# Delta path: keys before queries in the projection, and the scan's first steps of two tiles moved into it

## What is computed

```python
qkv = silu(short_conv(concat([dq, dk, dv]), conv_w))      # 5 taps along the tokens
qd  = l2_norm(heads(cq)) * DN_DK ** -0.5
kd  = l2_norm(heads(ck));  vd = heads(cv)
g    = -exp(a_log) * softplus(da + dt_bias);  beta = sigmoid(db)
# per chunk, for each head and direction
g = cumsum(g);  decay = exp(where(tril, g_i - g_j, -inf))
L = tril(einsum(k_beta, k) * decay, -1)
T = inverse(eye + L)                                      # unit lower triangular
a_intra = einsum(q, k) * decay
v_new = T @ v_beta - (T @ (k_beta * exp(g))) @ state
o     = (q * exp(g)) @ state + a_intra @ v_new
state = state * exp(g_last) + (k * exp(g_last - g)).T @ v_new
```

## Time and profile before

| what | us |
|---|---|
| median of 3 runs (3514.41 to 3517.09) | 3516.15 |
| the profiled execution, its own time | 3511.73 |
| span of that execution | 3509.9 |
| projection, group 0 (2111.8 to 2315.5) | 203.7 |
| scan, group 0, up to the recurrence of tile 0 (2315.6 to 2364.9) | 49.4 |
| one later step of the scan | 26.2 |
| projection, group 1 (2556.5 to 2754.1) | 197.6 |
| scan, group 1, up to the recurrence of tile 0 (2754.2 to 2803.7) | 49.5 |
| busy share of the span: PE, DVE, ACT, POOL | 87%, 59%, 39%, 32% |

### The profile page before, as it was taken

The page is one execution under the profiler, slowest core; times in us unless marked ns, Lnnn a source line. Parts: engine busy times, 40 slices in busy tenths (PEclk is TensorE's granted clock), DMA queues, the critical chain, the costliest instruction groups (busy, mean ns, idle before and its releaser), DMA issues. The chain is left out here.

```text
span 3509.9 us, 44499 instructions
## 1 busy us (share of the span) xinstructions
PE 3069.2 (87%) x16273; PEld 2501.5 (71%) x16273; DVE 2077.2 (59%) x3903; ACT 1377.7 (39%) x2733; POOL 1140.6 (32%) x1254
## 2 busy tenths in 40 slices
PE   5899988878998878899999999868878688899988
PEld 3578756756786657677887887758867588688777
DVE  6699775566997757766761015558755587101333
ACT  1366466124763651336652213434323443221222
POOL 2236321231562224421004332234423344424330
PEclk9999999999998999899999999989989799899999
DMA  6423332621233234310003123022231322512421
GB/s 213 123 79 94 94 96 76 205 104 45 79 97 129 85 113 152 116 37 1 1 10 102 48 83 102 26 76 76 55 109 30 76 80 52 162 48 97 142 96 43
DMA packets 227148, 303.15 MB, mean 86 GB/s; under 512 B 40912, under 2 KB 142032, under 8 KB 224754
## 3 DMA queue, kind: packets, MB, share of 16 engines
q1 hardware_dynamic: 215410, 279.33, 26.1%
q10 hardware_dynamic: 11520, 20.98, 1.6%
HBM read 241.91 MB, written 58.33 MB: 86 GB/s over the span
## 5 line engine op out<-in xcount | busy, mean ns | idle before, releaser
L816 PE MATMUL psum<-qs,hT 128*128 128x512 f32 x1344 | 308.3, 391 | 6.7 <-POOL qs L903 6.6
L816 PEld LDWEIGHTS psum<-qs,hT 128*128 128x128 f32 x1344 | 252.7, 189 | 62.2 <-issue 5.3
L2354 PE MATMUL psum<-bhsn,bringn 128*128 128x512 f32 x1152 | 264.8, 392 | 14.0 <-POOL bringn L2410 13.1
L2667 PE MATMUL psum<-hTs,cws 128*128 128x512 f32 x1056 | 261.0, 409 | 16.5 <-POOL hTs L2922 14.6
L2354 PEld LDWEIGHTS psum<-bhsn,bringn 128*128 128x128 f32 x1152 | 217.8, 189 | 61.0 <-issue 13.5
L2667 PEld LDWEIGHTS psum<-hTs,cws 128*128 128x128 f32 x1056 | 207.5, 198 | 61.4 <-POOL hTs L2922 15.0
L2354 PE MATMUL psum<-bhsa,bringa 128*128 128x512 f32 x1056 | 240.1, 389 | 2.8 <-POOL bringa L2410 2.8
L2354 PEld LDWEIGHTS psum<-bhsa,bringa 128*128 128x128 f32 x1056 | 198.2, 188 | 44.2 <-issue 3.2
L1583 PE MATMUL psum<-w_out,oys 128*128 128x512 f32 x768 | 180.8, 397 | 32.0 <-DVE w_out L1666 29.3
L1583 PEld LDWEIGHTS psum<-w_out,oys 128*128 128x128 f32 x768 | 146.4, 192 | 66.4 <-DVE w_out L1666 30.3
L983 DVE TENSOR_SCALAR_CACHE_REDUCE junk<-score,cand 128x384 uint8<-128x384 f32 x248 | 186.8, 810 | 2.2
(11 more groups left out here) (514 smaller groups left out, 7039.2 us busy)
## 6 DMA issues: line engine op xcount, KB each, us to landing
stg<-in_w_in SPq DMA_DIRECT2D x96, 256.0 KB, 2.7
score<-in_w_ada SPq DMA_DIRECT2D x32, 512.0 KB, 3.8
pj<-ptmp ACTq DMA_DIRECT2D x64, 256.0 KB, 2.1
dlb<-blocks SPq DMA_DIRECT2D x32, 512.0 KB
dlb<-in_w_in SPq DMA_DIRECT2D x22, 512.0 KB, 4.0
wa<-in_w_ada SPq DMA_DIRECT2D x8, 1024.0 KB, 8.3
oyf<-yTd SPq DMA_DIRECT2D x16, 512.0 KB, 6.2
ostg<-in_w_out SPq DMA_DIRECT2D x16, 512.0 KB, 5.6
```

Source lines behind the costliest of these rows:

```text
L816: mm = pe.matmul(bank(m), lhs, rhs, start=(kc == 0 and x == 0), stop=(kc == KC - 1 and x == 2))
L2354: mm = pe.matmul(ps[:, m, :], lhs[:, fs], h, start=(kc == 0 and x == 0), stop=(kc == KC - 1 and x == 2))
L2667: mm = pe.matmul(ps[:, u % 4, :], w, h, start=(kc == 0 and x == 0), stop=(kc == KC - 1 and x == 2))
```

## The change

1. The columns come in the order keys, queries, values (`KIND = (1, 0, 2)`), so what belonged to key columns 4 to 7 now happens four steps earlier, and the queries' squares go to a buffer of their own (`sqq`).
2. In group 0 the decay inputs are loaded after chunk 3 of the activations, split before the first column is copied out, and projected right after columns 0 and 1; their later steps use PSUM bank 7. The weights lie in a fixed place (`sc.jws`).
3. Keys of the first two tiles and queries of the first tile: Gram products, decays, `weigh`, `causal`, `decayed` and the block stores are made in columns 8 to 10 (`gram_keys` twice, `gram_queries` once). Only the queries' Gram product of tile 1 is left to the scan.
4. The first tile's substitution is made in the projection: steps 0 to 7 after column 10's `convolve`, steps 8 to 14 after column 11's.
5. The scan starts at `now = -1`; POOL clears T and X first, then widens; DVE's steps -1 and 0 have orders of their own. SP loads the blocks of tile 1 as its first DMAs of the scan.

```diff
@@ SP, stage_conv
                 if kc == 3:
                     sp.dma_start(taps5[:, :, :], ...
+                    if decays:
+                        prepare_decays()
-            if decays:
-                prepare_decays()
...
-            for r in range(2):
-                ...
-                store_blocks(sp, t, sc, 0, r, sc.NLT[0] if r == 0 else sc.NLx)
-                load_row(sp, t, sc, hg, 1, r)
-            sp.wait_ge(s_wlo, C - BASE)
-            for r in range(2):
-                load_blocks(sp, t, sc, 0, r, sc.Lb)
+            for st in range(2):
+                for r in range(2):
+                    load_row(sp, t, sc, hg, st + 1, r)
+                sp.wait_ge(sc.s_NLT, 2 * st + 1)
+                store_blocks(sp, t, sc, st, 0, NLTs[st][0])
+                sp.wait_ge(sc.s_NLx, st + 1)
+                store_blocks(sp, t, sc, st, 1, sc.NLx)
+                if st == 0:
+                    sp.wait_ge(s_wlo, C - BASE)
+                    for r in range(2):
+                        load_blocks(sp, t, sc, 0, r, sc.Lb)
@@ PE, stage_conv
             mm.then_inc(s_tT, 1)
+            if decays:
+                project_decays()
             for c in range(2, C + 2):
                 if c < C:
                     project(c)
+                if decays and c == 2:
+                    turn_decays()
+                if decays and c == 4:
+                    sum_decays()
+                if decays and c == 5:
+                    turn_cum()
                 after(c - 2)
-                if HG + 3 <= c < 2 * HG + 3:
-                    back(c - HG - 3)
+                if 3 <= c < HG + 3:
+                    back(c - 3)
+                if c == 8:
+                    for r in range(2):
+                        gram_keys(0, r)
+                if c == 9:
+                    for r in range(2):
+                        gram_queries(r)
+                if c == 10:
+                    for r in range(2):
+                        gram_keys(1, r)
@@ ACT, stage_conv
+            if decays:
+                split_decay_w()
             for c in range(C + 2):
+                if decays and c == 2:
+                    keep_decays()
+                if decays and c == 4:
+                    soft_decays()
+                if decays and c == 5:
+                    exp_decays()
+                if decays and c == 6:
+                    keep_rows()
...
-                if HG + 3 <= c < 2 * HG + 3:
-                    keep_k(c - HG - 3)
+                if 3 <= c < HG + 3:
+                    keep_k(c - 3)
+                if c in (7, 9):
+                    for r in range(2):
+                        decay((c - 7) // 2, r)
+                if c in (8, 10):
+                    for r in range(2):
+                        weigh((c - 8) // 2, r)
@@ DVE, stage_conv
             for c in range(C):
                 convolve(c)
...
+                if 2 <= c < HG + 2:
+                    normalise_k(c - 2)
+                if c in (8, 10):
+                    for r in range(2):
+                        decayed((c - 8) // 2, r)
+                if c == 9:
+                    for r in range(2):
+                        attend(r)
+                if c == 10:
+                    substitute(dve, sc, sc.Lb, 0, range(0, 8))
+            substitute(dve, sc, sc.Lb, 0, range(8, 15))
@@ stage_delta
-        TIMES = range(-3, NT + 1)
+        TIMES = range(-1, NT + 1)
@@ SP
+            for r in range(2):
+                load_blocks(sp, t, sc, 1, r, Lb[1])
             sp.dma_start(merge[:, :, :], t["c_merge"]).then_inc(s_m, 16)
...
-                if ahead(now + 2):
+                if now >= 0 and ahead(now + 2):
@@ PE
+                if now == -1:
+                    gram(1, 0)
+                    gram(1, 1)
@@ POOL
                 if now == -1:
+                    pool.wait_ge(s_X0, 1)
                     widen(0, 0)
                     widen(0, 1)
                     start_blocks(1)
+                    clear_states()
@@ DVE
                 if now == -1:
-                    substitute(0, range(0, 9))
+                    turn_first(0, 0)
+                    turn_first(0, 1)
+                    attend(1, 0)
+                    attend(1, 1)
+                    continue
+                if now == 0:
+                    solve_blocks(1, range(0, 3))
+                    merge16(0, 0)
+                    merge16(0, 1)
+                    decayed(2, 0)
+                    attend(2, 0)
+                    solve_blocks(1, range(3, 7))
+                    merge32(0, 0)
+                    merge32(0, 1)
+                    decayed(2, 1)
+                    attend(2, 1)
+                    solve_blocks(1, range(7, 15))
+                    turn_first(1, 0)
+                    turn_first(1, 1)
+                    continue
```

More of the change, by code:

```diff
@@ L2497, in __init__ @@
         self.Rb = [self.rows[:, r].rearrange("p (h q) -> p h q", h=HG) for r in range(2)]
+        self.NLT1 = [self.rows[:, 2].rearrange("p (h q) -> p h q", h=HG),
+                     k.sb(ctx, f"dnlt1_{hg}", [P, HG, P], side="right")[:, :, :]]
+        self.Tc = k.sb(ctx, f"dtc_{hg}", [P, 2, HG, 16], side="right")
+        self.part = k.sb(ctx, f"dpart_{hg}", [P, 2, HG, 15], side="right")
+        self.subs = 0
+        self.s_ti, self.s_sub, self.s_solved = (k.sem(n) for n in ("Tc_init", "subst", "solved"))
         (self.s_relu, self.s_dk, self.s_md, self.s_nbd, self.s_G, self.s_QK, self.s_NLT, self.s_NLx,
@@ L3069, in stage_delta @@
         gap, md, NLx = sc.gap, sc.md, sc.NLx
-        NLT = [sc.NLT] + [pair(f"dnlt{i}_", HG, P) for i in range(1, 3)]
+        NLT = [sc.NLT, sc.NLT1, pair("dnlt2_", HG, P)]
         AT = [sc.AT] + [pair(f"dat{i}_", HG, P) for i in range(1, 4)]
@@ L3666, in _ @@
                     attend(now + 2, 0)
[L3667 to L3673 removed]
+                if sub:
+                    solve_blocks(now + 1, range(0, 2))
                 if scan:
@@ L3678, in _ @@
                     attend(now + 2, 1)
-                if inv and now:
+                if inv:
                     merge16(now, 0)
@@ L3683, in _ @@
                     values(now - 1, 0)
-                if sub and now:
-                    substitute(now + 1, range(2, 6))
+                if sub:
+                    solve_blocks(now + 1, range(2, 6))
                 if inv:
@@ L3696, in _ @@
                 if sub:
-                    substitute(now + 1, range(6, 10))
+                    solve_blocks(now + 1, range(6, 10))
                 if scan:
@@ L3700, in _ @@
                 if sub:
-                    substitute(now + 1, range(10, 15))
+                    solve_blocks(now + 1, range(10, 15))
                 if scan:
```

291 lines of the change are left out of this document (146 added, 145 removed).

## The result

The changed kernel takes 3531.85 us (median of 6 runs, 3523.29 to 3535.0) against 3516.36 (6 runs, 3510.73 to 3525.79) for the kernel before, measured beside it: ratio 1.0044, 95% interval 1.0026 to 1.0061. It is slower, where 3504.0 and "faster" had been forecast, and it lies above the range of 3489 to 3515. The changed kernel was measured only then. The kernel before was measured again beside every set of experiments, with medians of 3518.32 (experiments 1 to 4), 3515.39 (5 to 7), 3513.31 (8 and 9) and 3517.66 (10), so a difference of totals between two such sets carries some 5 us of its own.

The account below looks back on a forecast made before the run. PE paces the projection; a chain of waits, paid once per group, sets the scan's start. Scan -20 (10 a group) plus projection +7.5 gives -12.5: 3511.7 to 3499.2, plus 4.4 for the median, 3503.7, so 3504; range 3489 to 3515.

Parts of the forecast that it names:

- rival 2: Projection: substitution meets POOL's power and scaling, costing 4.5 a group, 9 in all; total 3513, no change; chance 0.13.
- Rival 3: Projection: key columns become the bottleneck at 21.7 each against 18.2, +28 over eight columns; total 3528; chance 0.07.
- The step that failed: Scan start: `left` at S+11.4, tile 2's blocks first used at S+40.6, `right_side` at S+42.2 against S+51.4, 9.2 gained.
- Turned blocks: Scan start: tile 2's turned blocks end 13 after `left`, at S+24.4, then their stores and load follow on SP.
- their excess beyond 12.5: Scan start: tile 1's blocks land at S+10 to S+13 before `merge16`, costing nothing up to 12.5, only what exceeds it.
- The load: Scan start: tile 2's block load, issued at S+30.6, takes 10.0 to first use at S+40.6; other bound 13.2.
- The two steps: Scan start: two substitution steps in front of `right_side` on DVE hold it 1.6 more, to S+42.2.
- The 0.8 for the step behind it: Scan step after the start: shorter by 0.8, because PE has done early what DVE would have waited for.
- The weak end: Scan start: lower bound of the gain, 7 a group if the block load takes 13.2, against 10 forecast.
- The projection: Both groups' projections get longer: +3.0 in group 0 and +4.5 in group 1, +7.5 together.
- 0.4 net over both: Projection group 1: a query's square (1.06) on ACT in front of two `keep_k` costs 0.4 net of the old order.
- 1.0 on chunk 7: Projection group 0: decay inputs queued before chunks 4 to 7 delay the last, costing 1.0, between 0 and 2.

Follow-up runs that it names:

- experiments 1 to 4: Changed kernel with two tile 2 steps moved later, 3514.39 us; step 0 reordered on DVE, 3509.63; both, 3500.84; two query squares moved behind keep_k, 3523.83.
- 5 to 7: Changed kernel with tile 0's merges moved ahead, 3525.01 us; POOL's tile 0 products moved, 3519.01; block loads cut into smaller first parts, 3504.83.
- 8 and 9: Changed kernel with DVE reorder, later tile 2 steps, moved squares and cut loads, 3495.18 us; with DVE reorder and cut loads only, 3500.51.
- 10: Kernel before, without the change, with block loads cut into 2 x 128 KB and 2 x 384 KB: 3509.04 us, ratio 0.9975.
- Experiment 6: Changed kernel with POOL's three tile 0 products moved between tile 3's two causal masks in step 0: 3519.01 us, ratio to the kernel before 1.001.
- experiment 2: Changed kernel with DVE's merges and tile 2's products ahead of tile 1's substitution in step 0: 3509.63 us, ratio to the kernel before 0.9976.
- e4_square: Changed kernel with ACT's squares of the first two query columns moved behind the last two keep_k: 3523.83 us, ratio to the kernel before 1.0015.
- experiment 5: Changed kernel with only tile 0's two merges moved ahead of tile 1's first three substitution steps: 3525.01 us, ratio to the kernel before 1.0027.

## Why the prediction was wrong

**What held.** The scan's start is a chain of waits and not a full engine, `left` is at S+11.1 (11.4 forecast), the block load is the last link, and the two steps in front of `right_side` hand its lateness on. In the projection the substitution met no POOL (rival 2): it began at 2309.61 at 0.24 to 0.28 an operation, 4.5 after POOL's last there. (The quarter of its rate by which that rival was priced is not how the rows go: an operation that meets POOL waits for the product that is running, however short it is itself.) Rival 3 did not come true either: the key columns of group 0 are 19.4, 19.4 and 19.0 apart, above the 18.2 of before and below the 20.2 at which it decides; in group 1 they are 21.3, 15.5, 18.6 and 17.4, which is 18.2 in the mean. The wait of group 1's first key column was 6.16 (5.9 forecast), group 0's 2.13:

```profile
2633.84 1.94 PE L161 MATMUL psum<-cst,ccv 128*128 128x128 f32 x8 [6.16 <-DVE d_ktok L3073]
```

**The step that failed** is the sum from `left` to the first use of tile 2's blocks and the two steps behind it. The forecast made it 42.2 from S; it was 51.7. The 9.5 between them are three terms:

- *Turned blocks, S+24.4 in the forecast, S+29.7 measured: 5.3.* I took 13 from `left` and it was 18.6. The start of tile 1's steps was seen rightly ("land at S+10 to S+13", measured 13.0), and so was the rule ("in front of `merge16`", costing "their excess beyond 12.5"). But I priced three steps there at DVE's undisturbed rate. POOL's scaled copies, which had been waiting 3.69 for their own rows from DRAM, began 0.7 us after the blocks landed. The two arrive within 0.8 of each other: both loads are issued in the first 2.9 us of the scan. Experiment 6 puts 2.4 to 3.0 of the 5.3 on this; experiment 2, with all of tile 2's products ahead of substitution, takes the turned blocks to S+19.6. The other 2.3 or so I read from the rows, and no run takes them apart: PE's second `left` and `right` wait for `decayed(2, 0)` and run at the low clock, and `decayed(2, 1)` stood behind the transposes that wait for them. The order written by hand put the longest chain behind work that nobody was waiting for.
- *The load, 10.0 in the forecast, 12.6 measured: 2.6.* The forecast named 13.2 as the other bound and took the shortest row there was. Where DVE waits for the whole load of tile 2, it takes 10.2 to 13.7 in the kernels with the change and 10.0 and 11.4 in the kernel before.
- *The two steps, 1.6 in the forecast, 3.2 measured: 1.6.* Once more POOL's copies (2374.76), released by the landing of `decrow`, which is issued right behind the blocks. The row that warned of it was in hand (1.11 at 2390.07 in the earlier trace rows), was used against the projection (rival 2), and not here.

The 0.8 for the step behind it was not there either: from the first to the third `right_side` it is 27.8 in both.

**The bounds failed with it.** The weak end was 7 a group, from a slower load alone. Turned blocks and load late together was in no case that I wrote down, though a gain of 9.2 rested on a chain whose length I had put together from estimates. "SP: S+24.4" had no bound of its own. As a rival, "the new order delays tile 2's turned blocks until `right_side` is where it was" was missing: 0 a group, +7.5 in all, and that is within 2 us of what the two projections and the two starts show (+9.4). The other stretches show 4.6 more, which is within what they vary by.

**The projection** was forecast at +7.5 and was +9.1, the right size for partly the wrong reason, which is luck. The square of a query, "0.4 net over both", was the mis-sized term: taken away, it gave 2.2 a group in PE's waits, and 3.8 and 2.7 in the length of the stretches (the 0.4 was net of what the old order had there, which no run measures). In group 0 I had put the key columns at 0 and 1.0 on chunk 7, which was not late. What stays of the other terms once the squares are moved is 0.4 in group 0 and 2.2 in group 1 in e4_square, with the scatter named above.

The Trainium skill (GPSIMD Engine Reference, 8. Key points) was cited in the forecast for POOL and DVE sharing their SBUF interfaces. The trace of experiment 6 agrees: with POOL's copies moved away, the steps of 112 and 104 columns that had taken 0.99 to 1.23 take 0.27. What this kernel pays is the rest of POOL's product for each step that meets one.

**What stays open.** Why the whole load takes 10.2 in one kernel and 13.7 in another: row loads, stores of 4 KB and `decrow` are in the queue around it each time, and no run took one of them away. And the 6.8 us of experiment 5, of which the traces show 0.6.

## What to carry to other kernels

A prologue that is shortened hands its time to the next load of the same kind, so place that load in the new timeline with each instruction in front of it on each queue, and write the case "it ends where it ended before" down as a rival. On an in-order engine, put the operations that start a store, load and use chain ahead of those that nobody waits for yet, and keep the first users of a load out of the way of the recurrence until it has surely landed. Price an operation that can meet another engine's at the length of that engine's, and look for it wherever two loads land together. Where a wait on a large load cannot be hidden, load first what the first step reads: here one edit of a helper was worth 27 us, and a third of that without the change that had exposed it.

## What the runs showed of the hardware

A broadcast load of 2 x 512 KB from DRAM took 10.0 to 13.7 us from issue to first use where DVE waited for it; cut so that 2 x 128 KB come first, these took 4.4 to 7.4, at 0.62 us of SP's time for each further transfer (2.52 for four against 1.28 for two). The forecast had taken this way as a term that does not get shorter.

A multiply or an add of a substitution step, 0.2 to 0.28 alone, takes 1.0 to 1.3 in the rows shown when it begins beside a product of POOL of two SBUF tiles. It ends 0.07 to 0.14 behind that product, at 48 columns as at 112. The product itself hardly changes (1.27 alone, 1.30 beside them). DVE's products with one input in PSUM show none of this: in the changed kernel those of 2364.28 and 2365.99 take 0.69 beside POOL's scaled copies, as they do elsewhere.

PE's eight products of 128 columns took 2.08 behind waits of 5.24 and 6.90 us (the latter in e5_merge2) and 1.16 behind one of 1.36 (e6_pool2), against 1.06 in a running stretch, that is the 1.2 and the 2.4 GHz level; the granted clock of the first 49.6 us is 0.72. Behind the wait of 5.24 the eight after them took 1.92 as well. So a wait of five us on this path costs its own length and some 2 us more in the sixteen products behind it.
